# Block pairs of an FFN: two of four weight mixtures formed by a plain load and an accumulating DMA, all mixtures as sums

## What is computed

```python
def swiglu(x, g, w_gu, w_down):
    gu = rmsnorm(x, g) @ w_gu
    return (jax.nn.silu(gu[..., :D_FF]) * gu[..., D_FF:]) @ w_down
```

## Time and profile before

| | |
|---|---|
| median of 3 runs | 1291.03 us (1290.96 to 1292.95) |
| profiled execution, its own time | 1293.6 us |
| its span | 1291.9 us |
| granted clock of TensorE, mean | 0.995 |
| TensorE, VectorE, ScalarE, GpSimd busy | 98%, 63%, 46%, 3% |
| DMA moved | 114.9 MB, 89 GB/s over the span |

### The profile page before, as it was taken

How to read it: one execution, slowest core, us unless ns; L and a number is a source line. 1 busy time by engine, 2 the same in 40 slices (tenths; PEclk the granted TensorE clock), 3 DMA queues, 4 the chain that set the end, 5 groups by cost and what they waited for, 6 DMA issues and landing times. The chain is left out here.

```text
span 1291.9 us, 23175 instructions
## 1 busy us (share of the span) xinstructions
PE 1260.4 (98%) x9420; PEld 1218.7 (94%) x9420; DVE 819.5 (63%) x1344; ACT 589.3 (46%) x1078; POOL 37.8 (3%) x60
## 2 busy tenths in 40 slices
PE   6999999999999999999999999999999999999997
PEld 6998999999999999999998986799999999999997
DVE  4765557964885588654654466556874786378741
ACT  6656435431552255434663467534451454155421
POOL 1000000000000000002000100000000000000011
PEclk8999999999999999999999999999999999999999
DMA  6234122232323233324443320022233223223321
GB/s 214 83 117 131 33 82 82 66 101 80 96 85 99 65 99 98 98 82 131 130 115 101 102 70 2 2 82 82 66 105 89 75 85 111 86 75 99 115 77 46
DMA packets 201969, 114.92 MB, mean 89 GB/s; under 512 B 5035, under 2 KB 198219, under 8 KB 201864
## 3 DMA queue, kind: packets, MB, share of 16 engines
q1 hardware_dynamic: 197832, 101.24, 26.6%
q0 software_dynamic: 3840, 12.15, 2.5%
q10 hardware_dynamic: 192, 0.06, 0.0%
HBM read 106.54 MB, written 6.90 MB: 88 GB/s over the span
## 5 line engine op out<-in xcount | busy, mean ns | idle before, releaser
L961 ACT ACTIVATE WH<-RAW 128x1024 fp32r<-128x1024 f32 (+2 forms) x157 | 161.2, 1027 | 271.3 <-PE ACCP L1553 271.2
L1246 DVE TENSOR_TENSOR WL<-RAW,WH 128x1024 fp32r<-128x1024 f32 (+2 forms) x157 | 186.7, 1189 | 59.5 <-ACT WH L961 58.2
L1553 PE MATMUL ACCP<-FFNH,WH 128*128 128x288 f32 x704 | 151.1, 296 | 0.0
L1553 PE MATMUL ACCP<-FFNH,WL 128*128 128x288 f32 x704 | 150.8, 296 | 0.0
L1553 PE MATMUL ACCP<-FFNL,WH 128*128 128x288 f32 x704 | 147.7, 298 | 1.3
L1442 DVE TENSOR_TENSOR X<-X,ACCP 128x288 f32<-128x288 f32 x112 | 45.8, 450 | 136.1 <-PE ACCP L1553 136.0
L1561 PE MATMUL MISC<-BH,EH 128*128 128x288 f32 x400 | 118.5, 296 | 1.4 <-DVE EL L1273 1.4
L1561 PE MATMUL MISC<-BL,EH 128*128 128x288 f32 x400 | 118.0, 295 | 0.0
L1561 PE MATMUL MISC<-BH,EL 128*128 128x288 f32 x400 | 117.6, 294 | 0.0
L1553 PE MATMUL ACCP<-XH,WH 128*128 128x288 f32 x512 | 113.6, 304 | 3.7 <-DVE XL L1326 3.7
L1553 PEld LDWEIGHTS ACCP<-FFNL,WH 128*128 128x128 f32 x704 | 111.7, 189 | 4.0 <-DVE FFNL L1482 3.6
(11 more groups left out here) (266 smaller groups left out, 2845.1 us busy)
## 6 DMA issues: line engine op xcount, KB each, us to landing
RAW<-in_w_gu SPq DMA_DIRECT2D x88, 512.0 KB, 3.6
RAW<-in_w_down SPq DMA_DIRECT2D x32, 448.0 KB, 3.9
RAW<-in_w_in SPq DMA_DIRECT2D x16, 512.0 KB, 4.1
RAW<-in_w_mem_kv SPq DMA_DIRECT2D x16, 512.0 KB, 3.9
RAW<-in_w_out SPq DMA_DIRECT2D x16, 512.0 KB, 3.9
RAW<-in_w_down SPq DMA_DIRECT2D x16, 512.0 KB, 4.2
RAW<-in_w_kv SPq DMA_DIRECT2D x8, 512.0 KB, 3.6
XR<-in_x_prompt SPq DMA_DIRECT2D x4, 512.0 KB, 6.1
```

The source lines that it names most:

```text
L961: a.activation(WH[:, w % SPLIT_SLOTS, 0:nk, 0:ncol], RAW[:, p % RAW_SLOTS, 0:nk, 0:ncol], ACT.Copy).then_inc(split_ready(w, True)[0], 1)
L1246: v.tensor_tensor(WL[:, w % SPLIT_SLOTS, 0:nk, 0:ncol], RAW[:, p % RAW_SLOTS, 0:nk, 0:ncol], WH[:, w % SPLIT_SLOTS, 0:nk, 0:ncol], ALU.sub ...
L1553: ins_ = t.matmul(ACCP[0:ncol, s.g % 2, b, 0:c1_ - c0_], w[:, slot, k, 0:ncol], m[:, k, c0_:c1_], start=begin, stop=end)
```

## The change

For each pair that is not alone, SP loads only the second half of the up panel into RAW. It then waits until the first two low parts EL of the pair before are made, and loads the up panel's second half into SB[:, 0] and the gate panel's first half into SB[:, 1], 256 KB each. GpSimd waits for each of these and issues a DMA that adds the up panel's first half to it. `mix_1` and `mix_3` are left to the alone pairs. SB 1, SB 2 and SB 3 are sums now in place of differences; the signs of two terms of x and of the hidden product are turned to fit, with an instruction that takes a factor of -1. VectorE's `mix_2` waits for the first sum, ScalarE's first split for both.

```diff
--- before.py
+++ after.py
@@ -150,7 +150,7 @@
     steps = []
     count = {"panel": 0, "acc": 0, "job": 0, "sq": 0, "xs": 0, "ys": 0, "unit": 0, "normed": 0, "store": 0,
              "zero": 0, "win": 0, "r": 0, "h": 0, "rm": 0, "msq": 0, "pool": 0, "bank": 0,
-             "plain": 0, "split": 0, "pair": 0}
+             "plain": 0, "split": 0, "pair": 0, "added": 0}
     panel_shape, splits, raw_free = [], [], []
     units_before, sq_of_norm, branch_bank = {}, {}, {}
 
@@ -308,6 +308,8 @@
                 splits.append(("pair", p, i))
                 raw_free.extend([("pair", i)] * 2)
                 left = len(pairs) - 1 - n
+                added[i] = (take("added") if i != pair0 else None), mixes[0]
+                mixes[0] += 4 if i == pair0 else 2
                 add("pair", layer=layer, i=i, p=p, sn=w, view=gate_of(j), ys=up_of(j), slot=j - j0, h=layer * FC + j,
                     prev=steps_of_pair[i - 1] if n else None, nxt=left > 0, alone=i == pair0, bank=left % 2,
                     side=count["acc"] % 2, before=steps[-1] if i == pair0 else None, m=count["job"], g=count["acc"])
@@ -326,6 +328,7 @@
                     add("premix", i=count["pair"], p=count["panel"] + 2)
 
     steps_of_pair, rjob_of_lead = {}, {}
+    added, mixes = {}, [0]
     xsq_of = {}
     for layer in range(DEPTH):
 
@@ -668,6 +671,8 @@
         xc_hi, xc_lo = sem("xc_hi"), sem("xc_lo")
         pair_hi, pair_lo = sem("pair_hi"), sem("pair_lo")
         mixed, block_hi, block_lo = sem("mixed"), sem("block_hi"), sem("block_lo")
+        addend_loaded = [sem(f"addend_loaded{b}") for b in range(2)]
+        sum_loaded = [sem(f"sum_loaded{b}") for b in range(2)]
         block_done, copied = sem("block_done"), sem("copied")
         u_ready, up_right, crossed = sem("u_ready"), sem("up_right"), sem("crossed")
         gate_left = sem("gate_left")
@@ -822,12 +827,12 @@
 
         @block.sync
         def _(sp):
-            def load(p, src):
+            def load(p, src, k0=0):
 
                 nk, ncol = panel_shape[p]
                 if p >= RAW_SLOTS:
                     sp.wait_ge(*raw_released(p - RAW_SLOTS))
-                sp.dma_start(RAW[:, p % RAW_SLOTS, 0:nk, 0:ncol], src()).then_inc(raw_loaded[p % RAW_SLOTS], 16)
+                sp.dma_start(RAW[:, p % RAW_SLOTS, k0:nk, 0:ncol], src()).then_inc(raw_loaded[p % RAW_SLOTS], 16)
 
             for tt in range(TT):
                 sp.dma_start(XR[:, tt], x_prompt[0, tt * P:(tt + 1) * P]).then_inc(xin_loaded[tt], 16)
@@ -852,7 +857,13 @@
                                      YST[1][:, 0:TT]).then_inc(y_last_stored, 16)
                 elif s.kind == "pair":
                     load(s.p, s.view)
-                    load(s.p + 1, s.ys)
+                    if s.alone:
+                        load(s.p + 1, s.ys)
+                    else:
+                        load(s.p + 1, lambda: s.ys()[:, HK:KC], HK)
+                        sp.wait_ge(block_lo, 5 * (s.i - 1) + 2)
+                        sp.dma_start(SB[:, 0], s.ys()[:, HK:KC]).then_inc(addend_loaded[0], 16)
+                        sp.dma_start(SB[:, 1], s.view()[:, 0:HK]).then_inc(addend_loaded[1], 16)
 
 
         @block.gpsimd
@@ -928,6 +939,11 @@
                     gp.wait_ge(gate_steps, GATE_STEPS)
                     out(outs["fox_logf_prompt"][0].rearrange("(t p) h -> p t h", p=P), LG[:, 0, 0:TT], misc_stored)
                     out(outs["fox_logf_sample"][0], LG[0:LS, 0, TT], misc_stored)
+                elif s.kind == "pair" and not s.alone:
+                    n = added[s.i][0] + 1
+                    for b in range(2):
+                        gp.wait_ge(addend_loaded[b], 16 * n)
+                        gp.dma_start(SB[:, b], s.ys()[:, 0:HK], accum_op=ALU.add).then_inc(sum_loaded[b], 16)
                 elif s.kind == "project" and s.final and s.n < KC - 1:
                     yp = outs["y_prompt"][0].rearrange("(t p) d -> p t d", p=P)
                     cols = slice(s.n * P, (s.n + 1) * P)
@@ -972,7 +988,14 @@
 
             def mix_hi(i, first, n):
 
-                act.wait_ge(mixed, 4 * i + first + n)
+                summed, before = added[i]
+                if summed is None:
+                    act.wait_ge(mixed, before + first + n)
+                elif first == 0:
+                    act.wait_ge(sum_loaded[0], 16 * (summed + 1))
+                    act.wait_ge(sum_loaded[1], 16 * (summed + 1))
+                else:
+                    act.wait_ge(mixed, before + 2)
                 if i:
                     act.wait_ge(block_done, NB * (i - 1) + (6 if first + n > 2 else 3))
                 a.activation(EH[:, first:first + n], SB[:, first:first + n], ACT.Copy).then_inc(block_hi, n)
@@ -1255,17 +1278,24 @@
             def mix_3(i, p):
 
                 dve.wait_ge(*raw_there(p - 1))
-                v.tensor_tensor(SB[:, 1], raw_panel(p - 1)[:, 0:HK], raw_panel(p)[:, 0:HK], ALU.subtract).then_inc(mixed, 1)
+                v.tensor_tensor(SB[:, 1], raw_panel(p - 1)[:, 0:HK], raw_panel(p)[:, 0:HK], ALU.add).then_inc(mixed, 1)
 
             def mix_2(i, p):
 
-                dve.wait_ge(mixed, 4 * i + 1)
-                v.tensor_tensor(SB[:, 2], SB[:, 0], raw_panel(p - 1)[:, 0:HK], ALU.subtract).then_inc(mixed, 1)
+                summed, before = added[i]
+                if summed is None:
+                    dve.wait_ge(mixed, before + 1)
+                else:
+                    dve.wait_ge(*raw_there(p - 1))
+                    dve.wait_ge(sum_loaded[0], 16 * (summed + 1))
+                    dve.wait_ge(block_lo, 5 * (i - 1) + 4)
+                v.tensor_tensor(SB[:, 2], SB[:, 0], raw_panel(p - 1)[:, 0:HK], ALU.add).then_inc(mixed, 1)
 
             def mix_4(i, p):
 
-                dve.wait_ge(mixed, 4 * i + 3)
-                v.tensor_tensor(SB[:, 3], raw_panel(p - 1)[:, HK:KC], SB[:, 2], ALU.subtract).then_inc(mixed, 1)
+                summed, before = added[i]
+                dve.wait_ge(mixed, before + (3 if summed is None else 1))
+                v.tensor_tensor(SB[:, 3], raw_panel(p - 1)[:, HK:KC], SB[:, 2], ALU.add).then_inc(mixed, 1)
 
             def mix_lo(i, first, n):
 
@@ -1295,7 +1325,10 @@
                     dve.wait_ge(crossed, s.i + 1)
                 else:
                     dve.wait_ge(acc_free, s.g + 1)
-                v.tensor_tensor(FF_[:, s.slot], TG[:], TU[:], ALU.mult).then_inc(h_ready, 1)
+                if s.kind == "pair":
+                    v.scalar_tensor_tensor(FF_[:, s.slot], TG[:], -1.0, TU[:], ALU.mult, ALU.mult).then_inc(h_ready, 1)
+                else:
+                    v.tensor_tensor(FF_[:, s.slot], TG[:], TU[:], ALU.mult).then_inc(h_ready, 1)
 
             def take_lead(s):
 
@@ -1464,15 +1497,15 @@
                     left, right = slice(0, HALF), slice(HALF, T)
                     dve.wait_ge(xn_ready, KC * (s.layer + 1))
                     if s.k == 1:
-                        o = v.tensor_tensor(BT[:, 1], XN[0][:, :, right], XN[0][:, :, left], ALU.subtract)
+                        o = v.tensor_tensor(BT[:, 1], XN[0][:, :, left], XN[0][:, :, right], ALU.subtract)
                     elif s.k == 2:
                         o = v.tensor_tensor(BT[:, 2], XN[1][:, :, right], XN[0][:, :, right], ALU.subtract)
                     elif s.k == 3:
                         dve.wait_ge(xmixed, 4 * s.layer + 1)
-                        o = v.tensor_tensor(BT[:, 3], XN[1][:, :, right], BT[:, 1], ALU.subtract)
+                        o = v.scalar_tensor_tensor(BT[:, 3], BT[:, 1], -1.0, XN[1][:, :, right], ALU.mult, ALU.subtract)
                     else:
                         dve.wait_ge(xmixed, 4 * s.layer + 3)
-                        o = v.tensor_tensor(BT[:, 6], XN[1][:, :, left], BT[:, 3], ALU.subtract)
+                        o = v.scalar_tensor_tensor(BT[:, 6], BT[:, 3], -1.0, XN[1][:, :, left], ALU.mult, ALU.subtract)
                     o.then_inc(xmixed, 1)
                 elif s.kind == "prepare_lo":
                     dve.wait_ge(xc_hi, NB * s.layer + s.k + 1)
@@ -1481,8 +1514,6 @@
                     dve.wait_ge(hh_ready, s.h + 1)
                     v.tensor_tensor(FL_[:, s.slot], FF_[:, s.slot], FH_[:, s.slot], ALU.subtract).then_inc(hl_ready, 1)
                 elif s.kind == "premix":
-                    mix_1(s.i, s.p)
-                    mix_3(s.i, s.p)
                     mix_2(s.i, s.p)
                     mix_lo(s.i, 0, 2)
                     mix_4(s.i, s.p)
@@ -1509,9 +1540,6 @@
                     if s.prev:
                         split_lo(s.prev.sn + 2)
                         hidden(s.prev)
-                    if s.nxt:
-                        mix_1(s.i + 1, up + 2)
-                        mix_3(s.i + 1, up + 2)
                     if not s.alone:
                         mix_lo_22(s.i, up)
                     if s.nxt:
```

## The result

The changed kernel takes 1366.7 us (median of 4 runs, 1363.8 to 1370.8) against 1291.0 for the kernel before (1289.8 to 1293.0): ratio 1.0585, 95% interval 1.0571 to 1.0598. It is 5.9% slower, by 75.7 us; 1293.0 had been predicted, and the range ended at 1310. Its profiled execution took 1363.8 us, with a span of 1362.1.

A forecast was written before the change was run, and what follows sets the result against it. The prediction took TensorE's matmuls to bound the FFN. Profiled 1293.6 us + 2.0 for the alone pairs - 0 = 1295.6, less 2.6 to reach the runs' median, gave 1293.0 us; range 1290.3 to about 1310.

The forecast's parts named there:

- What bounds the kernel: FFN: bound by TensorE's matmuls, busy all 11.20 us of a steady pair; at most 5 us to gain in both layers.
- what is removed: 34 pairs lose two VectorE instructions, 41 us of VectorE time, worth nothing on the path.
- signs: Mixtures become sums, signs turned in hidden product and x: 0.06 us more per pair, 0 to 0.3 in all, taken as 0.
- The chain's allowance: Steady pair: the chain from EL 0,1 to the second sum may take 8.8 us without moving anything.
- The accumulate: GpSimd's adding DMA of 256 KB in each chain: taken as 4.1 us, from plain DMAs of 2.6 to 6.7 us.
- C: Length from the end of EL 0,1 to the second sum: 3.8 + 4.1 = 7.9 us, bounds 6.4 and 10.5.
- Rival 2: Steady pairs slower too, C over 8.8 plus what parts absorb: + 11 to + 43 us, 1302 to 1334; chance 0.22.
- Rival 1: Each accumulate takes its engine time twice, 0.9 us more; hidden in steady pairs, + 5.6 at alone pairs, 1296.6; chance 0.25.
- The alone pairs: Chain behind each layer's alone pair: allowed 7.2 us, takes 8.2, so 1.0 too late per layer, + 2.0 us.
- the starts of the parts: Premixes at the starts of the parts: sums by about 311.5, premix starts at 319.68, so nothing added.
- What would show it: Signs in steady pairs: accumulate 4.1 us if right; over 5.2, and pairs over 11.2 late in part 3, for Rival 2.

The follow-up runs named there:

- e11: Kernel before, plus in 30 pairs two GpSimd DMAs into a spare buffer whose contents nothing reads, 56 of 60 accumulating: 1290.3 us, ratio 0.9983.
- e1: Changed kernel with a second buffer for mixtures 0 and 1, used in turn, and their loads issued one pair earlier, ahead of the panels: 1289.5 us, ratio 0.9977.
- e4: Only the sign part of the change: all mixtures made on VectorE as sums, none of the new DMAs: 1293.1 us, ratio 1.0001 to the kernel before.
- e2: Changed kernel with GpSimd's accumulating DMAs made plain loads into the same bytes, without the add: 1295.2 us, ratio 1.0018 to the kernel before.
- e5: Changed kernel with only mixture 0 summed by DMA; mixture 1 formed on VectorE again from the full up panel: 1302.7 us, ratio 1.0077.
- e3: Changed kernel with SP waiting for both sums of a pair before loading the next panels: 1353.7 us, ratio 1.0469 to the kernel before.
- e8: Changed kernel with ten repeated matmuls of block 0 on TensorE ahead of each wait for EL 0: 1361.0 us, ratio 1.0533.
- e6: Changed kernel with accumulates reading the same bytes as 128 rows of 2 KB, from other weights: 1331.5 us, ratio 1.0299 to the kernel before.
- e7: Changed kernel with the up panel loaded whole and accumulates reading it from SBUF in rows of 2 KB: 1309.0 us, ratio 1.0121.
- e10: Changed kernel, one buffer and same DMAs, with mixtures 0 and 1 each split into high and low parts alone: 1314.3 us, ratio 1.0166.
- e9: Changed kernel with each accumulate covering 2 of 4 k-tiles, half the rows and bytes: 1305.0 us, ratio 1.0107 to the kernel before.

## Why the prediction was wrong

**What bounds the kernel; what is removed; signs.** Right. TensorE bounds it, the 41 us of VectorE are worth nothing on the path (e11 keeps them and takes 1290.3; e1 is without them at 1289.5), the signs cost nothing (e4).

**The chain's allowance.** Right. A pair allows 8.8 us: in e2, where TensorE sets the pace again, 8.8 us is what lies between EL 0,1 and the next EH, at 11.2 us a pair. The forecast had TensorE feel a late sum first at the fourth block, for EL 2,3. Once the chains are as long as here, most of the waiting is at the second block, for EL 0,1 (36.7 of 50.4 us).

**The accumulate: the step that failed.** It is the second term in "so C = 3.8 + 4.1 = 7.9 us, bounds 6.4 and 10.5". The first term was fair: in the chain above, GpSimd begins to issue the second accumulate 4.0 us after SP's first issue. From there to the landing the forecast took 4.1 us, with 6.7 as the bound from above. The median measured is 7.2, and C is 11.4. By the runs the miss has two parts. One accumulate by itself takes 4.9 to land, not 4.1 (e5, and the first one of each pair in after). The second of two takes 2.3 more, of which 0.9 is gone when the panels are kept away (e3); that the rest comes from the first accumulate being under way is likely, since with one accumulate it isn't there (e5). The working priced a single DMA and put nothing for the one ahead of it on the same queue. The bound of 6.7 was that of a single transfer too, four times as large but plain. An operation that no row shows was bounded by rows that lack what makes it dear: the add.

**Rival 2 was the case**, with a chance of 0.22 and a C worked out only up to 10.5. Its model comes close. With the measured C of 11.4 its own rule gives: part 3 7 x 2.6 - 3.7 = 14.5, part 2 6 x 2.6 - 3.7 = 11.9, part 1 4.2 + 2 x 2.6 = 9.4, together 35.8 in a layer, 71.6 in both, so 1362.6 us; 1366.7 was measured. Rival 1's point, that each accumulate costs its engine time twice, was true as a fact (2.17 against 0.88 us), but the engine time by itself costs nothing: in e1 and e11 it is there and the kernels lose nothing. The Trainium skill (Collectives: The Full Stack, Part 3) puts the adding step of a collective at half the rate of the copying one. Here, with rows of 512 bytes on both sides, an accumulate took 2.5 times the engine time of a copy (2.17 against 0.88 us), so the direction agrees and the factor is larger.

**The alone pairs and the starts of the parts.** In after the first chain of layer 0 runs from 245.09 to 256.6, C = 11.5, in place of 8.2. By the same allowance of 7.2 that is 4.3 us too late, where 1.0 was forecast. In layer 1 the chain runs from 969.96 to 980.89, C = 10.9, 3.7 too late. The premixes ahead of parts 2 and 3 cost nothing, as forecast: in layer 0 of after TensorE waits for no EL between 276.9 and 353.2 us, where part 2 starts, nor between 413.8 and 490.2, where part 3 does.

**The clock** was no step of the working. It is a mechanism that its list did not have. e8 gave back 5.7 us net, and what the clock costs by itself was not separated further.

**What would show it.** The closing lines named it: accumulates over 5.2 us in steady pairs, and pairs longer than 11.2. Both came.

## What to carry to other kernels

When a buffer exists once and is refilled by a chain of queues, write down the ring (load, add, split, free, load) and compare its length with the period; a second buffer can make even a dear link free, as e1 shows with the DMA engines busy for 86% of a pair. Price such a chain with every link it has: two DMAs in a row on one queue are two issues and two landings, and here the second landed 7.2 us after its issue where the first took 4.9. And an operation that the trace does not show needs a bound from above that reaches past its plain relatives.

## What the runs showed of the hardware

- An accumulating DMA of GpSimd, 256 KB in rows of 512 bytes (after), against the plain one (e2): 528 packets against 80, 1.30 us to issue against 0.75, 2.17 us of the 16 engines against 0.88. It lands after 4.9 us if it is the first of two or alone (e5), after 7.2 if it is the second; the plain ones take 3.3 and 3.5. With 128 rows of 2 KB (e6) it has 0.87 us of issue, lands after 5.2 (median of both) and takes 1.77 us of the engines.
- TensorE's granted clock fell to 0.50 within one wait of 3.6 us, and stayed there for some 5 us of the full work behind it.
- The tail of the kernel, from SP's last DMA to the end of the span, differs between kernels that end with the same stores, and it changed when e11 gave GpSimd's queue more to carry. SP's last issue and the span in the kernel before, then in e11:

```profile
core 0 of [0], span 1291.9 us
...
1284.75 0.39 SPq L851 DMA_DIRECT2D out_y_prompt<-YST  x1
```

```profile
core 0 of [0], span 1288.6 us
...
1283.90 0.39 SPq L863 DMA_DIRECT2D out_y_prompt<-YST  x1
```

The tail is 7.1 us in the first and 4.7 in the second. It was 8.5 and 8.6 us in e6 and e7, which have the same 13632 packets on q0, and 5.1, 5.0, 5.2, 5.1 and 5.4 in the change, e8, e3, e10 and e1, which have the same 39744; 7.2 in e4 with 3840 like the kernel before, 5.1 in e2 with 9280, 5.9 in e5 with 21792, 6.5 in e9 with 22336. Equal packets give tails within 0.4 us of each other, but more packets don't give shorter ones, and the cause stays open. It matters for the verdict on e1: of the 2.9 us by which its profiled span is below that of the kernel before, 1.8 are the tail. That leaves 1.1 us. But e11, which keeps all of the work on VectorE, has 0.9 us outside its tail as well, and e4, without any of the new DMAs, 0.6. So no gain from the work taken off VectorE is shown, even with the waits hidden.
